# A Strassen-split SwiGLU and a sparse-attention stage: one token low part moved from GpSimd to VectorE, an output sum moved ahead of weight sums, and the weight fill regrouped in pairs

## The reference

```
x = x + 0.5 * swiglu(rms_norm(x, g1), w_gate, w_up, w_down)     # D_FF = 2816
x = x + hybrid_mixer(rms_norm(x, gm), ...)                      # GLA | sparse attention | mLSTM, gated and summed
x = x + 0.5 * swiglu(rms_norm(x, g2), w_gate, w_up, w_down)
swiglu(x) = (silu(x @ w_gate) * (x @ w_up)) @ w_down
```

## Time and profile before

| | |
|---|---|
| Time of three executions | 2656.52, 2657.62 (median), 2659.61 us |
| Time of the profiled execution | 2658.68 us |
| Its span, first to last instruction | 2656.9 us |
| Granted TensorE clock, mean | 0.998 |
| TensorE busy | 2616.6 us, 98% |
| VectorE, ScalarE, GpSimd busy | 1459.5, 1264.1, 1178.4 us |
| HBM read | 234.81 MB |

### The profile page before, as it was taken

One profiled execution on the slowest core, in us unless ns is written; L12 is line 12 of the kernel. 1 busy time (PEld: TensorE's weight loads), 2 busy tenths in 40 slices (PEclk: granted clock), 3 DMA queues, 4 the chain that ended last, 5 costly groups with the idle time before them and its releaser, 6 DMA issues. The chain is left out here.

```text
span 2656.9 us, 41444 instructions
## 1 busy us (share of the span) xinstructions
PE 2616.6 (98%) x15716; PEld 2217.7 (83%) x15716; DVE 1459.5 (55%) x2227; ACT 1264.1 (48%) x2323; POOL 1178.4 (44%) x688
## 2 busy tenths in 40 slices
PE   7999999999999999999999999999999999999999
PEld 6899988766777788898989989887667778888998
DVE  7353573565656367363673535745665663773543
ACT  6454543645534336363464535335555344363543
POOL 4565644221322346564565655432123324465554
PEclk9999999999999999999999999999999999999999
DMA  4232323310211232232222332333012112232322
GB/s 147 96 111 96 104 96 111 111 48 29 72 60 60 83 111 101 95 109 98 96 96 97 110 111 85 107 103 111 33 41 72 60 60 89 104 106 95 112 96 95
DMA packets 38549, 240.46 MB, mean 91 GB/s; under 512 B 4320, under 2 KB 5600, under 8 KB 16352
## 3 DMA queue, kind: packets, MB, share of 16 engines
q1 hardware_dynamic: 36416, 233.85, 25.6%
q10 hardware_dynamic: 1952, 4.12, 0.5%
HBM read 234.81 MB, written 2.10 MB: 89 GB/s over the span
## 5 line engine op out<-in xcount | busy, mean ns | idle before, releaser
L351 POOL TENSOR_TENSOR wlo<-raw,whi 128x1024 fp32r<-128x1024 f32 (+1 forms) x310 | 689.2, 2224 | 1232.8 <-ACT whi L427 801.1
L1629 PE MATMUL bank<-hhi,whi 128*128 128x512 f32 x816 | 339.3, 416 | 15.7 <-DVE hlo L926 11.1
L427 ACT ACTIVATE whi<-raw 128x1024 fp32r<-128x1024 f32 (+1 forms) x198 | 192.7, 974 | 282.5 <-PE bank L1631 156.6
L1735 PE MATMUL bank<-th,slot_u 128*128 128x256 f32 x1152 | 326.0, 283 | 0.0
L1736 PE MATMUL bank<-tl,slot_u 128*128 128x256 f32 x1152 | 326.0, 283 | 0.0
L1631 PE MATMUL bank<-hhi,wlo 128*128 128x512 f32 x816 | 320.7, 393 | 0.0
L1630 PE MATMUL bank<-hlo,whi 128*128 128x512 f32 x816 | 319.7, 392 | 0.0
L1629 PE MATMUL bank<-ff,whi 128*128 128x512 f32 x704 | 274.0, 389 | 0.0
L1630 PE MATMUL bank<-ff,whi 128*128 128x512 f32 x704 | 274.0, 389 | 0.0
L1631 PE MATMUL bank<-ff,wlo 128*128 128x512 f32 x704 | 273.9, 389 | 0.0
L417 ACT ACTIVATE whi<-raw 128x1024 fp32r<-128x1024 f32 (+1 forms) x96 | 96.8, 1008 | 371.0 <-PE bank L1631 371.0
(11 more groups left out here) (348 smaller groups left out, 6271.3 us busy)
## 6 DMA issues: line engine op xcount, KB each, us to landing
raw<-cb SPq DMA_DIRECT2D x48, 768.0 KB, 4.2
raw<-gu0a SPq DMA_DIRECT2D x16, 1024.0 KB, 4.9
raw<-gu0b SPq DMA_DIRECT2D x16, 1024.0 KB, 4.9
raw<-pM SPq DMA_DIRECT2D x16, 1024.0 KB, 4.9
raw<-cq SPq DMA_DIRECT2D x16, 1024.0 KB, 4.9
raw<-gu1a SPq DMA_DIRECT2D x16, 1024.0 KB, 4.9
raw<-gu1b SPq DMA_DIRECT2D x16, 1024.0 KB, 4.9
raw<-gu0c SPq DMA_DIRECT2D x12, 1024.0 KB, 4.8
```

Of the source, the lines that this page charges most:

```text
L351: pool.tensor_tensor(wlo[:, s, 0:w], raw[:, j, lo:lo + w], whi[:, s, 0:w].bitcast(f32), ALU.subtract).then_inc(sem["lo_done"], 1)
L427: A(whi[:, s, 0:(wa, wb)[s]], raw[:, u % 2, s * wa:s * wa + (wa, wb)[s]], ACT.Copy).then_inc(sem["hi_done"], 1)
L1629: mm(outp, wh, mhi, start=start and k == 0, stop=False)
L1735: mm(outp, wh, parts[k][0], start=start and k == 0, stop=False, skip_group_check=True)
```

## The change

In the first unit of each SwiGLU, token low part 3 goes from GpSimd to VectorE, where it takes the place of the next unit's `block_sums`; these sums now stand behind the output sum L1089. TensorE waits for it on `t_low` in place of `t_lo`. Besides, the list `PM1` is rounded down to even numbers in slots 4 and on: the four query blocks have (0,2,0,2), (0,2,0,2), (2,0,2,0), (2,0,2,2) steps, still 72 a layer, and the slots after which a tile is through are the same as before.

```diff
-PM1 = ([4 * n if n < 4 else 16 + (n - 4) * 72 // 64 for n in range(69)], [KD * (i + 1) for i in range(11)])
+PM1 = ([4 * n if n < 4 else 16 + (n - 4) * 72 // 64 // 2 * 2 for n in range(69)], [KD * (i + 1) for i in range(11)])
...
                                 token_low(2)
                                 block_low(3, s3[:]).then_inc(sem["st_lo"], 1)
-                                token_low(3)
                                 block_low(6, s4[:]).then_inc(sem["lo_done"], 1)
...
+                def token_low(f, e):
+
+                    dve.wait_ge(sem["t_hi"], me.at("t_hi", 4 * f + e + 1))
+                    dve.tensor_tensor(tl[:, e], tf[:, e], th[:, e].bitcast(f32), ALU.subtract).then_inc(sem["t_low"], 1)
...
-                        if not end:
+                        if p == 0 and e == 0:
+                            token_low(f, 3)
+                        elif not end:
                             block_sums(u + 1, n + 1, False)
                         dve.wait_ge(sem["st_mm"], me.at("st_mm", 5 * n + 5))
                         dve.wait_ge(sem["st_snap"], me.at("st_snap", 3 * n + 3))
                         dve.wait_ge(sem["st_c"], me.at("st_c", 3 * n + 1))
                         dve.tensor_tensor(br[j][:, ST:S], bx[j], p7s[j], ALU.add).then_inc(sem["st_c"], 1)
+                        if p == 0 and e == 0:
+                            block_sums(u + 1, n + 1, False)
...
                     if first_t:
-                        pe.wait_ge(sem["t_lo"], me.at("t_lo", 2 * f + 2))
+                        pe.wait_ge(sem["t_low"], me.at("t_low", 3 * f + 3))
                     product(5, bw[j], t4, start=False).then_inc(sem["tile_done"], 1)
```

More of the change, by code:

```diff
@@ L242, in build @@
             "pre_hi": 3 * KD, "pre_lo": 3 * KD, "late_k": 3 * (KD - 1), "scaled": 10, "x_half": 12,
-            "t_sum": 8, "t_hi": 8, "t_low": 4, "t_lo": 4, "st_aps": 2 * NST, "st_sum": 8 * NST, "st_hi": 14 * NST, "st_low": 4 * NST,
+            "t_sum": 8, "t_hi": 8, "t_low": 6, "t_lo": 2, "st_aps": 2 * NST, "st_sum": 8 * NST, "st_hi": 14 * NST, "st_low": 4 * NST,
             "st_lo": 6 * NST, "st_mm": 10 * NST, "st_snap": 6 * NST, "st_c": 6 * NST, "st_silu": 4 * NST, "st_p": 2 * NST,
@@ L993, in norm @@
                         u, m, _ = strassen_units(f // 2, 0)[0]
-                        def token_low(e):
-                            dve.wait_ge(sem["t_hi"], me.at("t_hi", 2 * f + e + 1))
-                            dve.tensor_tensor(tl[:, e], tf[:, e], th[:, e].bitcast(f32), ALU.subtract).then_inc(sem["t_low"], 1)
                         dve.tensor_tensor(tf[:, 0], b11, b12, ALU.subtract).then_inc(sem["t_sum"], 1)
@@ L1008, in norm @@
                         block_sums(u, m, True)
-                        token_low(1)
+                        token_low(f // 2, 1)
                         block_low(2, m)
-                        token_low(0)
+                        token_low(f // 2, 0)
                         block_low(4, m)
@@ L1754, in block_unit @@
                     if first_t:
-                        pe.wait_ge(sem["t_low"], me.at("t_low", 2 * f + 1))
+                        pe.wait_ge(sem["t_low"], me.at("t_low", 3 * f + 1))
                     product(2, bx[j], t2, start=False).then_inc(sem["st_mm"], 1)
@@ L1758, in block_unit @@
                     if first_t:
-                        pe.wait_ge(sem["t_lo"], me.at("t_lo", 2 * f + 1))
+                        pe.wait_ge(sem["t_lo"], me.at("t_lo", f + 1))
                     if p == 0 and e < 2:
@@ L1764, in block_unit @@
                     if first_t:
-                        pe.wait_ge(sem["t_low"], me.at("t_low", 2 * f + 2))
+                        pe.wait_ge(sem["t_low"], me.at("t_low", 3 * f + 2))
                     product(4, bx[j], t1, start=False).then_inc(sem["st_mm"], 1)
```

## The result

The changed kernel takes 2681.4 us in the median of five executions (2680.8 to 2683.4), against 2657.6 for the kernel before on the same chip: a ratio of 1.0095, with a 95% interval of 1.0084 to 1.0106. That is 23.8 us slower; 21 had been forecast (2679). The profiled execution took 2680.8 us, with a span of 2679.0 against 2656.9.

The account below looks back on a forecast made before the run. TensorE, busy 98% of the span, was taken to bound the kernel through its order of work and waits. The profiled 2658.7 - 9.0 (first units) + 30.0 (paired fill) gave 2679.7, so 2679 us for the median, range 2670 to 2690.

Parts of the forecast that it names:

- What bounds: Whole run: TensorE, busy 98% of the span, sets the time; a change counts by what it does to TensorE's waits.
- The wait for L1089: First units: TensorE's wait for VectorE's output sum, four times, 7.5 us in all, goes whole.
- Priced at nothing: First units: later weight sums and GpSimd's lead cost nothing; if the cover failed, tenths of a us in four places.
- holds, by 0.7 us: First units: low parts ready near 74.6, before product 2 of the next unit wants them at 75.3.
- The half clock in place one: First of the four first units: clock at 0.50 after the idle time; its removal saves 1.5 us more.
- place one: The first of the four SwiGLU first units in a run, where 1.94 us idle and the clock's fall were read.
- part 1: First units, token low part and sums moved: -9.0 us, at worst -5, at best -9.5.
- The pairs: Attention fill in slots of two steps or none: +3.85 us per four query blocks, +30 in the run, bounds 23 to 38.6.
- The sum: Whole run: 2658.7 - 9.0 + 30.0 = 2679.7 us for the profiled execution; 2678.6, rounded 2679, for the median.
- The pairs did not gain: Rival, attention: transposes in slots without a step don't wait for the copy, 17 us gained, 2632; chance 0.06.
- The clock did not fall in the attention: Rival, attention: idle up to 0.94 us drops the clock, 16 falls of 1.5 us, 24 us, 2703; chance 0.07.
- part 1 gives nothing: Rival, first units: the wait moves by one product, 2688; chance 0.07.

Follow-up runs that it names:

- part1: Kernel before with only the first units changed (token low part 3 on VectorE, weight sums behind the output sum), fill as before: 2651.8 us, ratio 0.998.
- split: Kernel before with token low part 3 on VectorE and the weight sums cut in two around the output sum, fill as before: 2648.0 us, ratio 0.9965.
- part2: Kernel before with only the fill list PM1 rounded down to even numbers, first units as before: 2685.5 us, ratio 1.0109.
- bunch: Kernel before with all fill steps of a query block in its last slot, all else as before: 2739.6 us, ratio 1.0312.
- thirds: Kernel before with the fill dealt out by single matmuls to just fill each query block's ring, first units as before: 2646.6 us, ratio 0.9963.

## Why the prediction was right, and where not

**What bounds.** Right. All of the change is found in TensorE's waits and distances, and none of it in the shares of busy time: +29.2 us in the attention and -6.9 in the four first units make 22.3, and the two spans differ by 22.1.

**The wait for L1089.** Right: it is gone in the changed kernel and in `part1`, and VectorE reaches the sum at 68.42, as soon as product 4 is through. The new place of the token low part took 1.90 us (1.98 taken), and product 5 did not wait for it. GpSimd's low part 6 (63.55) stands before VectorE's sums (68.76), and no half clock follows the unit, as the prediction said.

**"Priced at nothing": wrong.** The step read that the weight sums now end later, that their low parts are wanted by product 2 of the next unit, and that this "holds, by 0.7 us". The low parts did hold (VectorE's two L1053 were not waited for). But I had followed the sums only on VectorE. On ScalarE the first of four high parts waits for the third sum; behind it stand, in ScalarE's order, the three others, the late silu, another high part, a block copy and then L549, and product 2 waits for that. It came 0.68 us late, four times: 2.7 us of the 9.0 given back. `split` won them back. The moved sums were followed along one of their two readers.

**The half clock in place one: read from one trace, and taken in full.** The 1.5 us were in the trace, and so was a longer wait in this place than three traces with the same first units show (`part2`, `bunch` and `thirds`: 0.6 to 0.8 us of wait and 19.6 to 19.8 us in place one, against 1.94 and 22.4). It should have been a bound and not a term. The granted clocks above speak against a single event, though: part of the executions of the kernel before have a lower mean clock than any of `part1`, so some of the term may be the change's. How much stays open. With both, part 1 is worth -4.9 us (-7.7 to -2.9) instead of -9.0, at the low end of its bounds, -5.

**The pairs.** Right, and by its steps. Second steps of +0.69, +0.65, +0.54 and +0.44 and slots without a step at the ring's period gave +3.85 us per four query blocks, less 0.1 a block 1 in the later pairs; measured are +1.36 (1.10 later), +0.63, +0.97 and +0.84, 3.8 in the first pair and 3.5 in the later ones. In all +29.2 against +30. The two that are low are block 3 (its last slot, without a step, is 1.07 and not 1.15 us) and the slot without a step of block 4 (1.37, not 1.41). TensorE's idle time in it is 0.78 us, where up to 0.94 was reckoned.

**The sum.** For the profiled execution 2679.7 was forecast and 2680.8 measured. Against the one trace of the kernel before, part 1 gave 6.9 of its 9.0 and the pairs cost 29.2 of their 30, which accounts for it. For the medians 2678.6 was forecast and 2681.4 measured: part 1 brought 4.1 less than its term, and the pairs cost 1.3 less than theirs. So the total is nearer than its larger error, because the two errors partly cancel; that much is luck.

**The rivals.** The pairs did not gain: the next transposes follow the copy's end, by 0.14 us, behind every slot without a step. The clock did not fall in the attention of the changed kernel: granted 1.00 in 548:690 and in 1875:2022. It did in `bunch`, with three slots without a step in a row, so the rival was a real mechanism whose point was not reached here. The Trainium skill's rule about short idle times between groups of matmuls ("TensorE: Matmul & The Clock Gate", section "A second HAM failure mode: psum-queue depth-cycling") fits `bunch`, where the clock fell in nine of 32 groups, and not the pairs, where it stayed at 1.00. That part 1 gives nothing was wrong, but it named the right kind of thing, the wait that moves by a product; a third of the gain of an undisturbed place went this way (0.68 of the 1.97 that product 6 had waited).

## What to carry to other kernels

Where two streams share an engine in order and one of them runs in a ring through a single buffer (here transposes, copy, transposes), the filler is worth most when each turn gets just as much as the ring leaves open: of two pieces in one turn the second covers nothing, and in the next turn, with none, the ring's wait stands open. Find the ring's period first, from a turn in which the wait is visible, then size the filler to it, in units finer than the natural one if need be. And when a producer is moved, follow every reader of what it makes through the in-order queue of that reader's engine to the next wait of the bounding engine, and let an event that one trace shows in one of four equal places be a bound, not a term. What would test the ring from its other side, a second buffer for the transposes, was not run.

## What the runs showed of the hardware

In `bunch` the granted clock fell to its half level in nine of the 32 groups, behind three slots with transposes alone. The idle stretches in them were 0.56 us long in four of the nine, 0.46 in one and 0.78 in four; eight groups with stretches of 0.67 had no fall. Single stretches of up to 0.78 us between full slots left it at 1.00 in the changed kernel. A fall cost 1.4 to 1.6 us in seven of the nine and near 3 in the two others. I had expected it only for idle times of the length of the earlier trace rows.

VectorE's token low part takes anything between 1.4 us (`thirds`) and 3.2 for the same work, and GpSimd's low part beside it stretches too. In the changed kernel, GpSimd in place one:

```profile
64.80 1.29 POOL L372 TENSOR_TENSOR slot_u<-raw,slot_u 128x512 fp32r<-128x512 f32 x1
...
66.52 1.80 POOL L372 TENSOR_TENSOR slot_n<-raw,slot_u 128x512 fp32r<-128x512 f32 x1 [0.43 <-ACT slot_u L544]
```

The second one overlaps VectorE's L1016 (65.27 to 67.17), and takes 0.5 us more than the first. It ends 1.15 us after VectorE's end, and VectorE's own ends 1.08 us after GpSimd's first one (66.09): each seems to run for a little over 1 us once the other is done. `part1` shows the same two times there: VectorE's (66.15 to 67.96) ends 1.08 us after GpSimd's before it, and GpSimd's next one 1.15 us after VectorE's. That they wait for each other is read from these times, not tested by a run. The Trainium skill, "SBUF — State Buffer", section "SBUF: two separate sides", says that a VectorE operation with two SBUF inputs and a GpSimd operation that reads SBUF exclude each other for a whole instruction; these rows agree. Moving a subtraction from GpSimd to VectorE therefore need not free GpSimd for its whole length: here 0.5 us of it came back, and 1.0 in `part1` (2.28 us for a low part of this size).

What stays open is why the start of the program differs by up to 1 us from kernel to kernel (TensorE's first wait is 10.3 to 11.2 us in these traces), and with it whether place one has its long wait and the half clock. No run was made on it.
